# PEER gates of two token blocks scattered by indirect stores instead of built from one-hot products

## What is computed

```
q = (xt @ w_query).reshape(T, H, 2, 128)                    # T = 512 tokens, H = 8 heads
s = einsum('thpd,hpkd->thpk', q, sub_keys)                  # scores of 2 x 128 keys
top_s, top_i = top_k(s, 16)
cand = top_s[:, :, 0, :, None] + top_s[:, :, 1, None, :]    # 256 candidates for each head
best_s, best_pos = top_k(cand, 16)
expert = top_i[.., 0] * 128 + top_i[.., 1] at best_pos      # of 16384 experts, 128 slots for each token
gate = softmax(best_s)
act = einsum('td,ted->te', x, u[expert])
out = einsum('te,ted->td', gelu(act) * gate, v[expert])
```

## Time and profile before

| what | value |
|---|---|
| median of three runs | 2816.7 us |
| profiled execution, its own time | 2817.84 us |
| its span, first to last instruction | 2816.2 us |
| mean granted TensorE clock | 0.975 |
| busy: TensorE, VectorE, ACT, POOL | 2660.4, 2014.0, 1292.6, 646.0 us |
| DMA queues: SP's, POOL's, ACT's share of 16 engines | 38.4%, 15.1%, 4.9% |
| HBM read, written | 539.6 MB, 68.2 MB |

### The profile page before, as it was taken

The page is one execution under the profiler, slowest core; times in us unless marked ns, Lnnn a source line. Parts: engine busy times, 40 slices in busy tenths (PEclk is TensorE's granted clock), DMA queues, the critical chain, the costliest instruction groups (busy, mean ns, idle before and its releaser), DMA issues. The chain is left out here.

```text
span 2816.2 us, 40392 instructions
## 1 busy us (share of the span) xinstructions
PE 2660.4 (94%) x14563; PEld 1353.1 (48%) x14563; DVE 2014.0 (72%) x3246; ACT 1292.6 (46%) x1379; POOL 646.0 (23%) x479
## 2 busy tenths in 40 slices
PE   6988999999999999999999889999999799999994
PEld 3464544444455554444444444455544455555552
DVE  4545778886688886888888854366543688888885
ACT  5432323323444444333333433344532488888884
POOL 0000000000001013888888300000000322332221
PEclk9988999999999999999999999999999799999997
DMA  5201334433375757999999622211214499999994
GB/s 194 105 31 45 113 113 157 149 143 149 142 224 179 223 180 265 346 364 366 364 364 368 260 105 105 87 63 61 75 60 150 175 387 397 398 400 400 394 400 152
DMA packets 129055, 609.08 MB, mean 216 GB/s; under 512 B 17328, under 2 KB 33712, under 8 KB 79296
## 3 DMA queue, kind: packets, MB, share of 16 engines
q1 hardware_dynamic: 57312, 411.62, 38.4%
q0 software_dynamic: 45024, 149.00, 15.1%
q10 hardware_dynamic: 26624, 47.19, 4.9%
HBM read 539.59 MB, written 68.16 MB: 216 GB/s over the span
## 5 line engine op out<-in xcount | busy, mean ns | idle before, releaser
L695 PE MATMUL ps<-a_hi,w_hi 128*128 128x512 bf16 (+2 forms) x1760 | 649.2, 371 | 11.8 <-ACT arena L1497 7.5
L696 PE MATMUL ps<-a_lo,w_hi 128*128 128x512 bf16 (+2 forms) x1760 | 649.0, 371 | 0.0
L697 PE MATMUL ps<-a_hi,w_lo 128*128 128x512 bf16 (+2 forms) x1760 | 648.6, 371 | 0.0
L695 PE MATMUL ps<-w_hi,arena 128*128 128x512 bf16 (+1 forms) x1600 | 610.0, 381 | 23.4 <-ACT arena L1609 14.6
L697 PE MATMUL ps<-w_hi,arena 128*128 128x512 bf16 (+1 forms) x1600 | 609.3, 381 | 0.0
L696 PE MATMUL ps<-w_lo,arena 128*128 128x512 bf16 (+1 forms) x1600 | 609.2, 381 | 0.0
L1917 DVE TENSOR_TENSOR w_lo<-w_st,w_hi 128x2048 bf16<-128x2048 f32 x127 | 290.9, 2290 | 177.1 <-ACT w_hi L1403 177.1
L1403 ACT ACTIVATE w_hi<-w_st 128x2048 bf16<-128x2048 f32 x127 | 242.3, 1908 | 318.3 <-PE ps L697 316.7
L1409 ACT ACTIVATE xn<-ps 128x512 f32<-128x512 f32 x128 | 76.4, 597 | 428.6 <-PE ps L697 428.6
L695 PEld LDWEIGHTS ps<-a_hi,w_hi 128*128 128x128 bf16 x1760 | 173.0, 98 | 196.3 <-ACT arena L1497 7.6
L697 PEld LDWEIGHTS ps<-a_hi,w_lo 128*128 128x128 bf16 x1760 | 172.8, 98 | 195.9 <-issue 3.5
(11 more groups left out here) (391 smaller groups left out, 3749.5 us busy)
## 6 DMA issues: line engine op xcount, KB each, us to landing
w_st<-in_w_all SPq DMA_DIRECT2D x260, 1024.0 KB, 6.7
arena<-in_w_all SPq DMA_DIRECT2D x64, 1024.0 KB, 9.3
act_dram<-xn POOLq DMA_DIRECT2D x64, 512.0 KB, 2.9
xn<-in_w_all SPq DMA_DIRECT2D x32, 1024.0 KB, 9.2
arena<-act_dram ACTq DMA_DIRECT2D x64, 384.0 KB, 5.3
gate_dram<-arena POOLq DMA_DIRECT2D x7, 3072.0 KB, 19.3
arena<-gate_dram ACTq DMA_DIRECT2D x64, 336.0 KB, 7.1
a_hi<-in_w_all SPq DMA_DIRECT2D x16, 1024.0 KB, 9.3
```

The costliest lines, as they stand in the source:

```text
L695: pe.matmul(dst, l_hi, r_hi, start=start, stop=False)
L696: pe.matmul(dst, l_hi, r_lo, start=False, stop=False)
L697: return pe.matmul(dst, l_lo, r_hi, start=False, stop=stop)
```

## The change

`unit_of(n)` sets in which chunk `n` a unit of scores is done: two units in chunks 0 and 1, then eight chunks with a unit and six without, three times. `last_unit_at(b)` is 9, 23 and 37 for blocks 1, 2 and 3. Softmax and slots follow each block. For blocks 1 and 2, VectorE computes for each slot the sum of the gates of all its token's slots with the same expert (`share`); a slot that an earlier head already has gets at least 1024 instead and is sent to a spare place behind the gates. `places` computes the address of each slot. POOL writes each column of 128 values, one for each token, with one indirect DMA (`spread`), six after each chunk's activations from chunk 16 on, 256 in all. Before that ACT has zeroed the matrix from a zeroed tile by four DMAs of 5.5 MB. Block 3 alone goes by one-hots: 16 gate tiles, one each in chunks 43 to 58, stored by two pairs of DMAs (after chunk 48 tokens 0 to 39, after 59 tokens 40 to 79; the last 48 stay in SBUF). `gate_dram` holds for each expert 336 gates in one run, and the loops over the chunks of this stage are written out.

The core of the diff, in this order: constants, POOL, TensorE, ACT in the query stage and in the expert stage, VectorE.

```diff
+GATE_TILES = [(0, t) for t in range(0, 40, 8)] + [(1, t) for t in range(80, P, 8)] + [(0, t) for t in range(40, 80, 8)]
+FIRST_TILE_AT = 43
+GATE_ROW = T_SPREAD + P - GT
+GATES = PK // 2 * P * 2 * GATE_ROW
+EARLIER = 1024.0
+PERIOD = 14
+SPREAD_FROM, SPREAD_PER_CHUNK = 16, 6
...
+def unit_of(n):
+    if n < PH - EARLY:
+        return EARLY + n
+    b, h = divmod(n - (PH - EARLY), PERIOD)
+    return PH * (b + 1) + h if b < TB - 1 and h < PH else None
...
+            def store_gates(tiles, first):
+                pool.wait_ge(g_out, 4 + 2 * tiles)
+                by_pair = g_st[:, 0, :, 0:40].rearrange("p (n j) t -> p j n t", j=2)
+                for j in range(2):
+                    at = j * GATE_ROW + T_SPREAD + first
+                    pool.dma_start(gate_rows[:, :, at:at + 40].rearrange("n p t -> p n t"), by_pair[:, j, :, :]).then_inc(g_stored, 16)
+            def spread(k):
+                b, j = divmod(k, SLOTS)
+                if j == 0:
+                    pool.wait_ge(place_done, b + 1)
+                pool.indirect_dma_start(gate_cells, bass.IndirectOffsetOnAxis(ap=place[:, b, j:j + 1], axis=0),
+                                        shared[:, b, j:j + 1], None).then_inc(g_spread, 16)
+            for n in range(N_U):
+                store_activations(n)
+                if n == FIRST_TILE_AT + 5:
+                    store_gates(5, 0)
+                if n == FIRST_TILE_AT + len(GATE_TILES):
+                    store_gates(len(GATE_TILES), 40)
+                if n >= SPREAD_FROM:
+                    for k in range(k, min(k + SPREAD_PER_CHUNK, 2 * SLOTS)):
+                        spread(k)
+                    k += 1
...
+            for n in range(N_U):
+                unit = unit_of(n)
+                if unit is not None:
+                    scores(unit, unit % PH, slice(unit // PH * P, (unit // PH + 1) * P))
+                expert_tile(n, 0)
...
+                if 0 <= at < len(GATE_TILES):
+                    gate_tile(at)
+                expert_tile(n, 1)
...
+                if m == 1:
+                    act.wait_ge(const_step, 4)
+                    cells = gate_dram[0:GATES].rearrange("(p a x) -> p a x", p=P, x=TB * SLOTS)
+                    for part in range(4):
+                        act.dma_start(cells[:, part * ZEROS:(part + 1) * ZEROS, :],
+                                      gate_t.unsqueeze(1).to_broadcast([P, ZEROS, TB * SLOTS])).then_inc(g_zero, 16)
...
+                if n == N_U - 2:
+                    act.wait_ge(g_stored, 64)
+                    act.wait_ge(g_spread, 16 * 2 * SLOTS)
+                    for r in range(2):
+                        load_experts(act, 0, r)
...
+            def share(b, h):
+                if h:
+                    dve.drain()
+                    dve.memset(weight[:, (h - 1) * PTOP:h * PTOP], EARLIER)
+                    dve.drain()
+                for j in range(h * PTOP, (h + 1) * PTOP):
+                    if j % SAME == 0:
+                        dve.drain()
+                    dve.scalar_tensor_tensor(same[:, j % SAME, :], expert, expert[:, j:j + 1], weight, ALU.is_equal, ALU.mult,
+                                             accum_out=shared[:, b - 1, j:j + 1])
...
+                for b in range(1, TB - 1):
+                    part = n - last_unit_at(b) - 3
+                    if 0 <= part < 4:
+                        share(b, 2 * part)
+                        share(b, 2 * part + 1)
+                        if part == 3:
+                            places(b)
```

More of the change, by code:

```diff
@@ L241, in build_program @@
         h_at = view(14 * 1024 + 5 * SLOTS, SLOTS)
+        spare = view(14 * 1024 + 6 * SLOTS, SLOTS)
+        late = view(14 * 1024 + 7 * SLOTS, SLOTS)
+        g_at = view(14 * 1024 + 8 * SLOTS, SLOTS)
+        move = view(14 * 1024 + 9 * SLOTS, SLOTS)
+        same = view(14 * 1024 + 10 * SLOTS, SAME, SLOTS)
         v_idx = sb("v_idx", [P, SLOTS], I32)
@@ L574, in _ @@
[L574 to L586, removed]
@@ L1440, in _, with gelu_tile @@
-            with act.Fori(4, 7) as i:
-                for c in range(8):
-                    experts_and_gates(i, c)
-            for c in range(8):
-                experts_and_gates(7, c)
-                if c == 6:
-                    act.wait_ge(g_stored[0], 16 * 5)
-                    act.wait_ge(g_stored[1], 16 * 4)
-                    for n in range(2):
-                        load_experts(act, 0, n)
+            def gelu_tile(n, t):
+                if t == 0 and n >= 2:
+                    act.wait_ge(u_stored[n % 2], 16 * (n // 2))
+                act.wait_ge(u_done, 2 * n + t + 3)
+                act.activation(u_st[:, n % 2, t, :], ps[:, t, :], ACT.Gelu).then_inc(u_out, 1)
@@ new lines, in gates_out @@
+            def gates_out(at):
+                b, first = GATE_TILES[at]
+                first -= 80 if b else first // 40 * 40
+                if at == 11:
+                    act.wait_ge(g_stored, 32)
+                for bank in range(2):
+                    act.wait_ge(g_done, 2 * at + bank + 5)
+                    tok = slice(first + bank * 4, first + bank * 4 + 4)
+                    act.activation(g_st[:, b, :, tok].rearrange("p k t -> p t k"),
+                                   ps[:, 2 + 2 * (at % 2) + bank, :].rearrange("p (t k) -> p t k", t=4), ACT.Copy).then_inc(g_out, 1)
@@ new lines, in _ @@
+            for n in range(N_U):
+                hi_in_loop(n, 16 * ((C_U + n + AHEAD) // RING + 1), u_done, 2 * n + 2)
+                gelu_tile(n, 0)
+                gelu_tile(n, 1)
+                if n in SOFT_AT:
+                    b = SOFT_AT[n]
+                    gates = gate_t[:, (b - 1 if b == 1 else b) * SLOTS:(b + 1) * SLOTS]
+                    act.wait_ge(soft_done, soft_shifted(b))
+                    act.activation(gates, gates, ACT.Exp).then_inc(soft_e, 1)
+                if n == FIRST_TILE_AT - 1:
+                    act.drain().then_inc(g_out, 4)
+                if 0 <= n - FIRST_TILE_AT < len(GATE_TILES):
+                    gates_out(n - FIRST_TILE_AT)
+                if n == N_U - 2:
[3 more added lines that the diff above has]
+                        load_experts(act, 0, r)
@@ new lines, in _ @@
+            for n in range(N_U):
+                unit = unit_of(n)
+                if unit is not None:
+                    dve.wait_ge(s_done, unit + 1)
+                lo_in_loop(n, C_U + n + AHEAD)
+                if unit is not None:
+                    best_keys(unit % PH)
+                    if unit % PH == PH - 1:
+                        b = unit // PH
+                        block_slots(b)
+                        if b:
+                            soft_start(0 if b == 1 else b, b + 1)
+                if n in SOFT_END_AT:
+                    b = SOFT_END_AT[n]
+                    soft_end(0 if b == 1 else b, b + 1)
+                    if b < TB - 1:
+                        share_start(b)
+                    else:
+                        rows_of_block_0()
+                for b in range(1, TB - 1):
[5 more added lines that the diff above has]
+                            places(b)
+                if n == TURN_AT + 1:
+                    slots()
+                if 0 <= n - FIRST_TILE_AT < len(GATE_TILES):
+                    gate_one_hots(n - FIRST_TILE_AT)
```

291 lines of the change are left out of this document (124 added, 167 removed).

## The result

The changed kernel takes 2963.1 us (median of four runs, 2956.6 to 2964.3) against 2817.4 for the kernel before on the same chip (four runs, the three of the table above among them): **5.1% slower**, a ratio of 1.0514 with a 95% interval of 1.0497 to 1.0531. The forecast was 2806, with a range of 2787 to 2865. The profiled execution took 2956.57 us, its span is 2954.9, so the spans differ by 138.7 us.

The account below looks back on a forecast made before the run. TensorE was taken to set the changed stage's pace. Terms -29 + 6 + 2 + 7 + 3 = -11 us took the profiled 2817.8 to 2806.8, the median to about 2806; range for 8 in 10, 2787 to 2865.

Parts of the forecast that it names:

- The gate tiles taken away: Expert stage on TensorE: 32 of 48 gate tiles and six of nine transposes removed, -29.0 us together.
- 11.25 from 43 to 58: Activation stores in chunks 43 to 58, each with a gate tile, were to come 11.25 us apart.
- Zeroing: Query stage: four DMAs on ACT's queue writing 22.0 MB were to cost nothing; +30 if ACT were held.
- VectorE's sums: Share instructions in chunks 12 to 15 and 26 to 29, delaying scores of chunks 18 and 32: +6 us, 0 to 38.
- The worked bound of 0.30: VectorE's share instructions in four chunks were to be free up to 0.30 us each; 0.32 was taken.
- POOL's stores: 256 indirect stores, six per chunk in chunks 16 to 58, mostly hidden behind TensorE: +2 us, +240 at 1.94 each.
- d = 0.94: Time in us of one indirect store on POOL, taken from gathers; free up to 0.99.
- Rival 2: POOL paces chunks 16 to 58 and the kernel is slower: 64 us at 1.24 per store, 2864; chance 0.24.
- Rival 3: DMA queue paces: each indirect store waits for its writes' receipt before the next moves; +168, near 2955; chance 0.06.
- Block 3's stores: Two pairs of gate-store DMAs at chunks 48 and 59, ahead of later activation stores in the same queue: +7 us.
- The clock: TensorE's granted clock drops after idle gaps, 1.7 us lost each; two such: +3 us.
- The sign named for a wrong forecast: Steps between activation stores 16 and 42, other than 18 and 32, taking over 10.8 us.

Follow-up runs that it names:

- the version that loses nothing else: Changed kernel with gate tile after both tiles, one-hots before w_lo, zeroing in 12 parts on POOL, gate stores one by one: 2787.0 us.
- the runs with the ring open: Changed kernel with one-hots written before the remainder of the weights, 2840.0 us; changed kernel with gate tile after both tiles, 2829.7 us.

## Why the prediction was wrong, point by point

**The gate tiles taken away: right.** 29.0 us forecast, 28.2 in the steps of the version that loses nothing else.

**"11.25 from 43 to 58": the step that failed.** The sum had one gate tile of 0.89 us added to TensorE's 10.36 and nothing for the wait before it. That the one-hots and evictions which fall away are no gain was right ("Both had idle time, so neither counts as a gain"); but the sixteen tiles that stay got a new place in three engines' orders, and it was put at nothing without being followed. In the kernel before, VectorE writes the one-hots of the chunk's first gate tile ahead of w_lo, and TensorE takes that tile right after tile 0 (the loop over `t` in the listing above); in the changed one w_lo is ahead, w_lo is released by w_hi, and w_hi comes behind the GELU of tile 1 of the chunk before. The durations needed are all in the trace of before: GELU 0.60, two evictions 1.9, w_hi 1.9, w_lo 2.29, one-hots 1.2 and 3.7, products 0.89, half a chunk 5.2. Their sum, 17.7 us against 11.25, is a forecast of 16 x 6.4 = 103 us more, and the clock adds to it. It measured 136.9. No rival held it either: two spoke of loads on an engine or a queue, two of how much stays hidden, none of a ring in which no engine is busy all the time. The range missed for that reason alone: 2963.1 less 136.9 is 2826, and the runs with the ring open measure 2840 and 2830, all inside 2787 to 2865. With 103 us, and up to the 2.7 us a chunk for the clock that only the runs show, the forecast of 2806 would have become 2909 to 2952.

**Zeroing: 0 taken, +26.4 measured** (30.0 against the version with the zeroing on POOL). The alternative had been written down at +30, for an ACT held until each transfer had drained, and was near: ACT is held for 44 us, three quarters of 60, though each issue returns before the transfer ahead of it has landed (the third starts at 317.5 us, the first lands at 325.7). The 2 us per issue for ACT came from no row; the row of ACT's 52.5 idle us is cover for the evictions but not for the splits of weights, which TensorE needs once per chunk with a ring of four. The share of the DMA engines, on which most of that paragraph is spent, turned out to be no cost at all (1.02, TensorE full).

**VectorE's sums: +6 taken, 1.4 measured.** The place was right and the size too large: TensorE waits before the scores of chunks 18 and 32, but 0.44 and 0.92 us instead of 3 each. The lower end was near: 0.27 us a sum, so an accumulator adds about 0.01 to the 0.263 of the earlier trace rows; its read is an instruction of 0.08 us that overlaps the next sum. The worked bound of 0.30 was a little too generous, since 0.27 should have left 3 us to spare.

**POOL's stores: +2 taken, 0 measured.** d = 0.94 was taken; the median is 0.962, with one of 1.9 to 2.9 beside w_lo in nearly every chunk. Beside VectorE's searches and even beside its sums of two inputs (0.35 us each) they stay at 0.96 to 1.1. The rule that was weighed there, from the Trainium skill, "SBUF — State Buffer", on who interferes with whom, is borne out where it was asked: the store that starts at 946.27 under the w_lo of 946.09 ends at 949.21, 0.83 after w_lo does. Rival 2 falls with it, and its working is confirmed by the doubled stores. Rival 3 falls as well: without the indirect stores nothing gets faster. Three slips in that working change no result: 54 of the 128 gathers of the earlier trace rows take 2.5 us or more, not one in four; 20 stores at 0.3 us are 6 and not 7; and 0.54 + 0.30 + 6 x 0.30 + 1.7 is 4.34, not 4.31.

**Block 3's stores: +7 taken, 7.7 measured** at the second pair, for a reason half seen: POOL stands before the second issue until the first transfer has landed (the times are in the last section). That the number fits is luck: +6 was the price of either pair, and the first, with the slow chunks around it, cost nothing. With fast chunks it can: with the one-hots first GELU waits at both pairs, and TensorE for it, 11.1 us in two waits.

**The clock: +3 taken for two gaps, far more in the runs.** After a wait of 6 us the products of tile 1 start 0.43 us apart instead of 0.22 and take 0.63 us each instead of 0.38 (955.33 above), which is the 1.2 GHz level, and later in the tile they are back at 2.4. Of a ring of 20.1 us, TensorE's part is 8.8 (953.2 to 962.0) where 0.89 + 5.2 = 6.1 would do: 2.7 us for each wait, an estimate for a chunk like this one. Sixteen of them are 43 us, and with the 96 us of waits before gate tiles that is 139, where 136.9 were measured.

The sign named for a wrong forecast, steps over 10.8 us between chunks 16 and 42, did come true, but it has nothing to do with the miss: it looked at the wrong stretch and at the wrong mark. Such steps are there: 17.3 us between stores 16 and 17, where POOL waits for the first places and then works off six stores, 11.0 at chunk 23, 11.6 and 11.5 near chunk 32. But steps of 9.2 to 9.9 follow, POOL catches up inside its two buffers, and TensorE, with 1.4 us of waits, none of them for POOL, never sees it. A store's start marks TensorE's pace only while POOL is idle before it. The 11.25 from 43 to 58 was the claim that broke.

## What to carry to other kernels

When an edit moves an operation in one engine's program, write out the ring it becomes part of, across all engines, from an output back to itself, and add up its durations before looking at any busy share. A ring costs when its sum is above the pace of the bounding engine, though no engine in it is busy all the time (here TensorE for 221 of 320 us, and the others less); it is opened by moving one member ahead of a wait that it doesn't need, on any one of the engines. And here large DMAs belonged on a queue whose engine had nothing due: what they cost was not bandwidth but the work behind their issue.

## What the runs showed of the hardware that was not expected

- Four DMAs of 5.5 MB (5376 KB in the page's table of issues) held ACT's sequencer for 44 us, issued one after the other; the same four took GpSimd 5.7 us.
- Zeroing and weight loads together at 405 GB/s, DMA share 1.02, did not slow TensorE in the query stage: it was busy for 40 of 40 us.
- A second DMA of 8,192 runs of 160 bytes right behind the first kept GpSimd waiting for 12.9 and 13.9 us before it was issued; put a chunk later it still waited, for 4.1 and 7.2. Where the trace has the landing of the first, the second is issued 0.4 to 0.9 us after it (with the gate tile last: landed at 948.1 and 1075.6, issued at 948.9 and 1076.0).
- An indirect store of 128 x 4 bytes to HBM takes GpSimd 0.96 us with 0.30 between two, near the 0.94 of the gather of the earlier trace rows.
- `DVE_READ_ACCUMULATOR` takes 82 ns and lies beside the next instruction, where ACT's takes 0.19 us.
